# The MLP stage of a hybrid decoder layer: gate and embedding products split in three, streamed as pieces, placed in the next chunk's up stage

## The reference, cut to what matters

```
h  = h + rmsnorm(mix, g_mix_post)
hn = rmsnorm(h, g_mlp_pre)
m  = square(relu(hn @ w_up)) @ w_down        # 1024 -> 4096 -> 1024
h  = h + rmsnorm(m, g_mlp_post)
gate = sigmoid(h @ w_ple_gate)               # 1024 -> 1024
e    = p @ w_ple_proj                        # 256 -> 1024
out  = h + rmsnorm(gate * e, g_ple_post)
```

## Time and profile before

| | |
|---|---|
| time, median of 3 runs | 3360.23 us (3358.62 to 3362.65) |
| profiled execution, own time | 3354.67 us |
| its span, first to last instruction | 3353.1 us |
| TensorE busy in the span | 3053.1 us (91%) |
| VectorE, ScalarE, GpSimd busy | 50%, 40%, 10% |
| mean granted TensorE clock | 0.947 |
| MLP stage, first up product to the end | 1575.8 to 3353.1 us |

### The profile page before, as it was taken

The page is one execution under the profiler, slowest core; times in us unless marked ns, Lnnn a source line. Parts: engine busy times, 40 slices in busy tenths (PEclk is TensorE's granted clock), DMA queues, the critical chain, the costliest instruction groups (busy, mean ns, idle before and its releaser), DMA issues.

```text
span 3353.1 us, 38038 instructions
## 1 busy us (share of the span) xinstructions
PE 3053.1 (91%) x13944; PEld 2353.3 (70%) x13944; DVE 1684.7 (50%) x3373; ACT 1334.7 (40%) x2162; POOL 336.3 (10%) x431
## 2 busy tenths in 40 slices
PE   5999968788888888996999989999999999999998
PEld 4877856565666776884788847888568886588873
DVE  3376777777866777631333343333433333433333
ACT  3253455756656477553322223222232222222221
POOL 1332322121120310000000000000000000000000
PEclk9999989798887878998999999999999999999999
DMA  3111142111201110105423303233123322133210
GB/s 118 60 53 57 36 124 58 53 52 35 62 20 30 45 35 22 54 23 186 136 90 101 120 31 119 88 101 120 48 79 113 101 89 94 58 119 101 88 50 26
DMA packets 215456, 250.92 MB, mean 75 GB/s; under 512 B 57952, under 2 KB 160096, under 8 KB 215264
## 3 DMA queue, kind: packets, MB, share of 16 engines
q1 hardware_dynamic: 212960, 239.99, 22.5%
q10 hardware_dynamic: 2304, 8.39, 0.6%
HBM read 208.34 MB, written 40.01 MB: 74 GB/s over the span
## 4 chain that ended last, share of the span: by engine, by line
issue 59%; PE 26%; DVE 7%; ACT 4%; POOL 2%; DMA 1%; SPq 0%; DVEq 0%; POOLq 0%; ACTq 0%
PE bank L1579 7%; PE bank L1721 6%; PE bank L1701 5%; PE bank L1601 2%; PE bank L1687 2%; PE bank L1602 2%; ACT kept L912 2%; DVE kept L1230 1%; DVE probs L1368 1%; ACT probsT L1015 1%; ACT score_tail L912 1%; DVE too_few L1238 1%; POOL rstdC L847 1%; POOL score L823 1%; PE bank L1550 1%
## 5 line engine op out<-in xcount | busy, mean ns | idle before, releaser
L1443 DVE TENSOR_TENSOR w_lo<-w_raw,w_hi 128x1024 fp32r<-128x1024 f32 x256 | 312.6, 1222 | 520.5 <-ACT w_hi L1058 514.8
L1058 ACT CAST w_hi<-w_raw 128x1024 fp32r<-128x1024 f32 x256 | 267.4, 1045 | 562.0 <-PE bank L1579 535.0
L1701 PE MATMUL bank<-values,probsT 128*128 128x64 f32 x2176 | 334.7, 301 | 149.7 <-ACT probsT L1015 124.6
L1701 PEld LDWEIGHTS bank<-values,probsT 128*128 128x128 f32 x2176 | 313.7, 219 | 176.7 <-ACT probsT L1015 162.8
L1579 PE MATMUL bank<-hn_hi,w_hi 128*128 128x512 f32 x1024 | 400.3, 391 | 14.9 <-DVE hn_lo L1460 10.7
L1579 PE MATMUL bank<-w_hi,hid_lo 128*128 128x512 f32 x1024 | 405.9, 396 | 0.0
L1579 PE MATMUL bank<-w_lo,hid_hi 128*128 128x512 f32 x1024 | 405.9, 396 | 0.0
L1579 PE MATMUL bank<-w_hi,hid_hi 128*128 128x512 f32 x1024 | 405.9, 396 | 0.0
L1579 PE MATMUL bank<-hn_lo,w_hi 128*128 128x512 f32 x1024 | 399.7, 390 | 0.0
L1579 PE MATMUL bank<-hn_hi,w_lo 128*128 128x512 f32 x1024 | 399.4, 390 | 0.0
L1368 DVE CUSTOM_DVE_ANT_0 probs<-bank,mask 128x384 f32<-128x384 f32 (+3 forms) x320 | 193.7, 607 | 234.4 <-PE bank L1602 232.3
(11 more groups left out here) (191 smaller groups left out, 4754.4 us busy)
## 6 DMA issues: line engine op xcount, KB each, us to landing
w_raw<-in_w_up SPq DMA_DIRECT2D x64, 1024.0 KB, 5.6
w_raw<-in_w_down SPq DMA_DIRECT2D x64, 1024.0 KB, 5.0
x_in<-in_x SPq DMA_DIRECT2D x16, 512.0 KB, 3.7
q_t<-q_scratch SPq DMA_DIRECT2D x32, 256.0 KB, 3.7
x_t<-in_x SPq DMA_DIRECT2D x16, 512.0 KB, 4.3
h_scratch<-h_t SPq DMA_DIRECT2D x16, 512.0 KB, 2.9
hnT_scratch<-hn2T_t SPq DMA_DIRECT2D x16, 512.0 KB, 3.9
hn_lo<-hnT_scratch SPq DMA_DIRECT2D x4, 2048.0 KB, 11.3
```

The costliest lines, as they stand in the source:

```text
L1058: nc.scalar.copy(w_hi[:, p % 4, :].rearrange("p (k f) -> p k f", f=piece_width(p)), raw_piece(p)).then_inc(w_hi_rdy, 1)
L1443: nc.vector.tensor_tensor(out_p, raw_piece(p), hi_p.bitcast(F32), ALU.subtract).then_inc(w_lo_rdy, 1)
L1701: last = nc.tensor.matmul(bank[:, 4, h * HEAD:(h + 1) * HEAD], probsT[:, m % 3, a * P:(a + 1) * P], values[:, kt, HEAD * kv:HEAD * (kv + 1 ...
```

## The change

`w_ple_gate` and `w_ple_proj` no longer lie in SBUF. Their products are split in three as well: the gate in eight pieces (four for each output half), the embedding in two, all through `w_raw`, `w_hi`, `w_lo`, for each chunk again. h3T and pT become hi and lo parts of the whole chunk. ScalarE and VectorE share their evacuation. A chunk's tail stands in the next chunk's first quarter, between its up and its down stage: 8 up pieces, then 8 gate and 2 embedding pieces, then 8 down pieces. The squares, means, scalings and transposes of h stand between the first up pieces. The transposes of p move into the last down stage of their own chunk, and so does the split of the next chunk's input. The addition of y to h2 moves from VectorE to GpSimd. All gate products of a half come before the sigmoids, all embedding products of a half before the gatings; the output is made in place. p and h2 are loaded in the third quarter. All four chunks are written out on all engines. The last chunk's tail stands alone at the end (`last_tail`).

```diff
-    PIECES = 2 * FT
+    GATE = 8
+    TAIL = GATE + 2
+    PIECES = NCH * (2 * FT + TAIL)
...
+        SIDE = ((4, 5, 6, 7), (0, 1, 2, 3))
+        H3 = ((4, 5), (6, 7), (2, 3), (4, 5))
+        H3_LAST = ((0, 1), (2, 3), (0, 1), (2, 3))
...
 SyncE
-                    if first and s == 1:
-                        for k in range(K):
-                            sp.dma_start(w_gate_sb[:, k, :], w_ple_gate[0, k * P:(k + 1) * P, :]).then_inc(wc_ld, 16)
...
+            def load_raw(width, src):
+                n = loads[0]
+                loads[0] += 1
+                if n >= 2:
+                    sp.wait_ge(w_lo_rdy, 2 * (n - 2) + 2)
+                sp.dma_start(w_raw[:, n % 2, :].rearrange("p (k f) -> p k f", f=width), src).then_inc(raw_ld[n % 2], 16)
...
+            for c in range(NCH):
+                for q in range(QUARTERS):
+                    if q == 2:
...
+                        sp.dma_start(p_in[:], p[0, 0, bass.ts(c, CH), :].rearrange("(a q) d -> q a d", q=P)).then_inc(p_ld, 16)
+                        sp.dma_start(h2[:], h2_dram[bass.ts(c, CH), :].rearrange("(a q) d -> q a d", q=P)).then_inc(h2_ld, 16)
...
+                    for n in range(4):
+                        load_up(q, n)
...
+                    if c > 0 and q == 0:
+                        load_tail()
+                    for n in range(4):
+                        if (q, n) == (QUARTERS - 1, 3) and c + 1 < NCH:
+                            sp.wait_ge(piece_done, up_piece(c, q, QF - 1) + 1)
+                            sp.dma_start(hn_lo[:].bitcast(F32), hnT_dram[:, :, bass.ts(c + 1, CH)]).then_inc(hn2T_ld, 16)
+                        load_down(q, n)
+            load_tail()
...
 GpSimd
+            def add_mlp(c, a):
+                pool.wait_ge(h2_ld, 16 * c + 16)
+                pool.wait_ge(mlp_scaled, CT * c + a + 1)
+                nc.gpsimd.tensor_tensor(h2[:, a, :], h2[:, a, :], y[:, a, :], ALU.add).then_inc(h3_rdy, 1)
+            for c in range(NCH):
+                root_C(c, 0)
+                for a in range(CT):
+                    if a + 1 < CT:
+                        root_C(c, a + 1)
+                    add_mlp(c, a)
...
 ScalarE
+            def up_stage(c, q):
+                seam = q == 0 and c > 0
+                for f in range(QF):
+                    p = up_piece(c, q, f)
+                    split(p + AHEAD)
+                    if seam and f < 2:
+                        square_mlp(c - 1, 2 * f)
+                        square_mlp(c - 1, 2 * f + 1)
+                    if seam and f >= 4:
+                        turned_h3(c - 1, f - 4)
...
+            def gate_stage(c):
+                for d in range(GATE):
+                    split(gate_piece(c, d) + AHEAD)
+                    if d == GATE // 2:
+                        sigmoids(c, 0)
+                for half in range(2):
+                    split(embed_piece(c, half) + AHEAD)
+                    if half == 0:
+                        sigmoids(c, 1)
...
+            def last_tail(c):
+                split(gate_piece(c, 3))
+                for a in range(CT):
+                    square_mlp(c, a)
+                for a in range(CT):
+                    turned_h3(c, a)
+                split(gate_piece(c, 4))
+                split(gate_piece(c, 5))
+                sigmoids(c, 0)
+                for d in range(6, TAIL):
+                    split(gate_piece(c, d))
+                sigmoids(c, 1)
+                for a in range(CT):
+                    square_gated(c, a)
+                for a in range(CT):
+                    store_out(c, a)
...
 VectorE
+            def turned_h3(c, a):
+                for n, b in enumerate(h3_banks(c, a)):
+                    dve.wait_ge(h3T_hi_rdy, 2 * (CT * c + a) + n + 1)
+                    part = slice(4 * n, 4 * n + 4), slice(a * P, (a + 1) * P)
+                    nc.vector.tensor_tensor(h3T_lo[:, part[0], part[1]], split4(bank[:, b, :]),
+                                            h3T_hi[:, part[0], part[1]].bitcast(F32), ALU.subtract).then_inc(h3T_lo_rdy, 1)
+            def up_stage(c, q):
...
+                    split(up_piece(c, q, f) + AHEAD)
+                    if f == 0 and (c, q) != (0, 0):
+                        evacuate_down(*((c, q - 1) if q > 0 else (c - 1, QUARTERS - 1)), 1)
+                    if seam and f in (1, 2):
+                        mean_C(c - 1, 2 * f - 2)
+                        mean_C(c - 1, 2 * f - 1)
+                    if seam and f >= 4:
+                        turned_h3(c - 1, f - 4)
...
+                    if seam and 1 <= f < 1 + CT:
+                        scale_mlp(c - 1, f - 1)
+            def gate_stage(c):
+                for d in range(GATE):
+                    split(gate_piece(c, d) + AHEAD)
+                for half in range(2):
+                    split(embed_piece(c, half) + AHEAD)
+                    if half == 1:
+                        gated(c, 0)
+            def down_stage(c, q):
+                for d in range(QF):
+                    split(down_piece(c, q, d) + AHEAD)
+                    if q == 0 and c > 0:
+                        if d == 0:
+                            gated(c - 1, 1)
+                        if 1 <= d < 1 + CT:
+                            mean_C(c - 1, CT + d - 1)
+                        if 2 <= d < 2 + CT:
+                            output(c - 1, d - 2)
...
+            def last_tail(c):
+                evacuate_down(c, QUARTERS - 1, 1)
+                split(gate_piece(c, 3))
+                for a in range(CT):
+                    mean_C(c, a)
+                    scale_mlp(c, a)
+                    if a > 0:
+                        turned_h3(c, a - 1)
+                turned_h3(c, CT - 1)
+                for d in range(4, TAIL):
+                    split(gate_piece(c, d))
+                for half in range(2):
+                    gated(c, half)
+                for a in range(CT):
+                    mean_C(c, CT + a)
+                    output(c, a)
...
 TensorE
+            def up_stage(c, q):
...
+                    if q == 0 and c > 0 and 3 <= f < 3 + CT:
+                        transpose_h3(c - 1, f - 3)
+            def down_stage(c, q):
...
+                    if q == 0 and c > 0 and d % (QF // 2) == 0:
+                        pe.wait_ge(ge_rdy, 2 * CT * (c - 1) + CT * (half + 1))
...
+                    if (q, d) == (QUARTERS - 1, 5):
+                        transpose_p(c)
+            def gate_product(c, p, d, a):
+                for r in range(2):
+                    k = 2 * (d % (GATE // 2)) + r
+                    h3_a = [part[:, k, a * P:(a + 1) * P] for part in (h3T_hi, h3T_lo)]
+                    last = split_product(bank[:, SIDE[d // (GATE // 2)][a], :], h3_a, halves((w_hi, w_lo), p, r, 512),
+                                         k == 0, k == K - 1)
+                return last
...
+            for c in range(NCH):
+                for q in range(QUARTERS):
+                    up_stage(c, q)
+                    if q == 0 and c > 0:
+                        gate_half(c - 1, 0)
+                        gate_half(c - 1, 1)
+                        embed(c - 1, 0)
+                        embed(c - 1, 1)
+                    down_stage(c, q)
+            transpose_h3(NCH - 1, 0)
+            for a in range(CT):
+                if a + 1 < CT:
+                    transpose_h3(NCH - 1, a + 1)
+                first_gate_half(NCH - 1, a)
+            gate_half(NCH - 1, 1)
+            embed(NCH - 1, 0)
+            embed(NCH - 1, 1)
```

More of the change, by code:

```diff
@@ L204, in hybrid_block @@
         p_in = sbC("p_in", [P, CT, PLE])
[L205 to L206 removed]
+        pT_hi = sbC("pT_hi", [P, KP, CH], F32R)
+        pT_lo = sbC("pT_lo", [P, KP, CH], F32R)
+        ssC = sbC("ssC", [P, 2 * CT])
         msC = sbC("msC", [P, 2 * CT])
         rstdC = sbC("rstdC", [P, 2 * CT])
[L210 to L218 removed]
         mlp_stack.close()
@@ new lines, in up_stage @@
+            def up_stage(c, q):
+                seam = q == 0 and c > 0
+                for f in range(QF):
+                    split(up_piece(c, q, f) + AHEAD)
[6 more added lines that the diff above has]
+                        turned_h3(c - 1, f - 4)
+                    F = FT * c + QF * q + f
+                    dve.wait_ge(relu2_step, 2 * F + 2)
+                    nc.vector.tensor_copy(hid_hi[:, f, :], square[:, f % 2, :]).then_inc(hid_step, 1)
+                    dve.wait_ge(hid_step, 2 * F + 1)
+                    nc.vector.tensor_tensor(hid_lo[:, f, :], square[:, f % 2, :], hid_hi[:, f, :].bitcast(F32),
+                                            ALU.subtract).then_inc(hid_step, 1)
+                    if seam and 1 <= f < 1 + CT:
+                        scale_mlp(c - 1, f - 1)
@@ L1540, in _ @@
+            split(0)
+            split_input(0, range(HN))
+            for n in range(1, AHEAD):
+                split(n)
+            for c in range(NCH):
+                for q in range(QUARTERS):
+                    up_stage(c, q)
```

(4 more changed lines are left out.)

536 lines of the change are left out of this document (261 added, 275 removed).

## The result

The kernel after takes 3247.18 us (median of 4 runs, 3245.62 to 3250.37) beside 3359.43 us (3356.34 to 3362.65) for the kernel before in the same session: ratio 0.9669, 95% interval 0.9657 to 0.9681. The profiled executions have spans of 3243.8 and 3353.1 us, 109.3 apart.

A forecast was written before the change was run, and what follows sets the result against it. TensorE was taken as the bound, with 10 idle us a seam from dependencies. Seams -78.4, last chunk's p +1.0, start -3.6 - 1.7, last tail +3.3: 3360.2 - 79.4, rounded 3281 us; ranges 3272 to 3291 and 3270 to 3298.

The forecast's parts named there:

- Gate and embedding operands have the shapes of down operands, so I price them at the down pace: Gate and embedding products split in three: 0.234 us an instruction, 5.62 us a piece, ten pieces 56.2 us a seam.
- Seams: Between chunks: TensorE never waits, 104 us from last down to next first down product; three seams 78.4 us less.
- h of tile 0: In a seam: ready at 18.2 us if each GpSimd addition holds VectorE, ahead of its transposes at 21.8.
- Transposes: Groups of eight in TensorE's product stream: 1.0 us each, own range 0.9 to 1.6.
- The clock (rival 2): Transposes amid products drop TensorE to 1.2 GHz: 26 to 52 us over 15 groups, say 3315 us; chance 0.04.
- Start: Chunk 0's start: TensorE's stall behind a late load goes, 3.6 us less, and p_in out of the way, 1.7 less.
- The 1.7 us for p_in: At the start: p_in's 0.5 MB no longer stands ahead of hn_lo and the first weights, 1.7 us less.
- Last tail: After the last down product: no up products cover it and two chains are longer, 97.5 us, 3.3 us longer.
- Rival 4: Whole kernel: more gain, p_in's bytes and a warm tail give 8 us more, 3271 us; chance 0.07.
- Rival 5: Seams keep their idle 10 us and only products get cheaper: 3321 us; chance 0.03.
- Rivals 1 and 3: Seams: 1, hidden handoffs cost 2 to 7 us each, 3293 us, 0.15; 3, late h3 chain, 3370 us, 0.03.
- the margins of under 1 us: End of a seam: VectorE's 4.9 us beside 5.62 us of embedding half 1, margin 0.7 us, first down product doesn't wait.

The follow-up runs named there:

- b_hid4096: Kernel before with three small tensors (88 bytes) put behind the hidden rows, which start 96 bytes lower: 3333.85 us, ratio 0.9916.
- a_add_dve: Kernel after with the addition of y to h2 back on VectorE, right behind the scaling: 3241.71 us, ratio 0.9655.
- a_tails_apart: Kernel after with every chunk's tail run by itself behind its last down product, in the last tail's order: 3311.51 us, ratio 0.9863.
- a_w32: Kernel after with w_hi and w_lo alone moved 32 bytes off a multiple of 64: 3292.75 us, ratio 0.9809.
- a_hid32: Kernel after with 32 bytes of padding ahead of hid_hi and 32 behind hid_lo; pT also moved 64 bytes against the weights: 3270.49 us, ratio 0.9738.
- a_all32: Kernel after with 32 bytes left free ahead of all MLP tensors, so every operand moves up together: 3247.65 us, ratio 0.9664.
- s_hid: Kernel after with the hidden rows at another offset in each of the 16 quarters: 3258.63 us, one run.

## Why the prediction was wrong

The direction and the mechanism hold; the size does not, and the runs name the term.

- **"Gate and embedding operands have the shapes of down operands, so I price them at the down pace"**, and with it the down pace itself, which the sum left as it was. This is the step that failed, a term of the sum that was mis-sized. The shapes are the same, but the pace is one of addresses, and the diff moves those. At 0.234 us the sum was true for the addresses of before; at 0.2267 it loses 16 x 1.45 + 40 x 0.18 = 30.4 us more, against a miss of 30 in the spans. That the two agree so closely is partly luck: the other errors cancel. The transposes took 1.8 us less than forecast and the last tail 2.5 less beyond its pace, and the start was 4.9 us worse (1.7 that were not there, and 3.2 of a late beginning). b_hid4096 shows the larger part by itself: 26 us (0.9916) from 88 bytes moved in the kernel before, where 23 follow from the stages. The rows for it were there: an up piece at 5.44 us and a down piece at 5.62, both of 24 instructions of one shape at granted clock 1.00. The prediction worked out both and never asked why they differ.
- **Seams.** TensorE never waits, as forecast. 101.5 us instead of 104: ten pieces at 0.18 less make 1.8, and the four groups of transposes 4 x 0.11 = 0.4. h of tile 0 was forecast at 18.2 us into the seam, with VectorE held for each addition; that addition ended 18.1 us in, ahead of transposes at 21.8. The time was right, the way to it was not: in the seam it was GpSimd that waited for VectorE's split.
- **Transposes** were priced at 1.0 us a group, the duration of a group in the seam of before, where a wait follows it; in the stream a group costs 0.89. Sixteen groups: 1.8 us.
- **The clock (rival 2)** did not fall: 1.00 with four groups of transposes in each seam of the kernel after. The Trainium skill (TensorE: Matmul & The Clock Gate, Part 4: PE-mode transpose) does not count transposes as work for the clock; groups of 0.79 us each among products show no fall, so here the rule changed nothing.
- **Start.** The stall of TensorE went, as forecast: chunk 0 is 8.5 us shorter, of which 4 x 1.45 are the pace, and of the remaining 2.7 the stall gives 3.5 and p's transposes, now in the stream, take 0.9. The 1.7 us for p_in were not there. The stage began 3.2 us later than before; in other runs of these kernels its first up product lies between 1575.8 and 1586.6 us, nearly all from work ahead of the MLP, which the change does not touch. What moves it stays open.
- **Last tail.** 93.2 us instead of 97.5. The pace gives 1.8 of the difference, outputs at 3.27 instead of 3.45 us another 0.7; the first gate product, forecast 18.5 us behind the first evacuation, came at 17.3 (1.2). The two stops ahead of it were as forecast. GpSimd's addition made 5.3 of their 13.7 us (a_add_dve), and the lock is seen in 3.35 us for a scaling of 1.28. The Trainium skill (SBUF — State Buffer, Who interferes with whom) calls it an exclusive lock, in which the one that starts second waits; the trace agrees in both directions, for GpSimd waits where VectorE began first (in the second seam VectorE's split began at 2351.31, the addition at 2351.53, and that took 3.25 us, beside 2.34 in the tail).
- **Rivals.** Rival 4 had the right sign of the miss, but for causes that were not there. Rival 5, products only, was put at 40 us slower than the forecast, with the 10 idle us of the old seam; a_tails_apart, the nearest run to it, has 16 idle us a tail and was 64 us slower than the kernel after. Rivals 1 and 3 saw no late handoff: the margins of under 1 us held.
- **Range.** The prediction names two, 3272 to 3291 and 3270 to 3298; the measured time lies below both. The range was built from the unknowns of the change and took the price of a product, the largest term, as known, since a row showed it. The row showed it for one layout.

## What to carry to other kernels

When two stages with the same instruction shapes at the same clock run at different paces, the difference is itself a finding: look where their operands start before pricing anything by either. Compare the addresses of both builds whenever a diff adds, drops or reorders tensors, and keep the two operands of TensorE's products at a distance of a multiple of 256 bytes, which was the fastest in every run here; small tensors go behind the large ones. A chain of handoffs costs nothing inside a stream that doesn't need it, and its full length where the stream ends, so look for independent work to put at that place.

## What the runs showed of the hardware

- The pace of a 128 x 128 held, 512 wide streamed fp32r product at granted clock 1.00 depends on the distance in SBUF from its streamed to its held operand, with a period of 256 bytes, at the multiples of 32 bytes that were run: 0.2267 us at 0, 0.2289 at 192, 0.2324 at 128, 0.2333 at 32, 64, 160 and 224, 0.2342 at 96. Up, down, gate and embedding products were slow alike when the weights moved by 32 (a_w32), and embedding products at 64 had 0.2333 as well (a_hid32). Their absolute place didn't matter (a_all32). At 16 bytes six pieces ran at 0.2267 and the two behind a group of transposes at 0.2333 (s_hid).
- Eight transposes in a running stream of products cost 0.89 us, 0.79 of them up to the next product's start, and the granted clock stayed at 1.00; behind a wait of 4.99 us, 1.6 us from 3166.56 to the product at 3168.18.
- When VectorE works on two large SBUF operands and GpSimd adds two others, the second waits for the first: a scaling goes from 1.28 to 3.35 us, an addition on GpSimd from 2.34 to 3.25. Behind products that hide the chain this costs nothing; in the last tail it cost 5 us together with the slower addition of GpSimd.
